# A hybrid transformer on one core: a changed order of routing, splits and the overflow branch, and constant matmuls at the experts' end

## The reference

```python
for i in range(DEPTH):                       # two layers
    mix = token_mixers(x, ...)               # x @ w_in, differential attention, attention over
                                             # the top 64 keys by an index score, gates, w_out
    x = layer_norm(ALPHA * x + mix, ln1_g[i], ln1_b[i])
    ffn = hierarchical_moe(x, ...)           # 4 groups of 8 experts; 2 experts of one group a token
    ple = jax.nn.sigmoid(x @ w_ple_gate[i]) * (p[i] @ w_ple[i])
    x = layer_norm(ALPHA * x + ffn + ple, ln2_g[i], ln2_b[i])
```

## Time and profile before

| | |
|---|---|
| median of 3 runs | 2013.76 us (2011.25 to 2013.92) |
| the profiled execution, its own time | 2016.33 us |
| its span, first to last instruction | 2014.2 us |
| PE busy | 1908.9 us (95%) |
| VectorE busy | 1406.5 us (70%) |
| ScalarE busy | 1073.4 us (53%) |
| mean granted clock of PE | 0.975 |

### The profile page before, as it was taken

The page is one execution under the profiler, slowest core; times in us unless marked ns, Lnnn a source line. Parts: engine busy times, 40 slices in busy tenths (PEclk is TensorE's granted clock), DMA queues, the critical chain, the costliest instruction groups (busy, mean ns, idle before and its releaser), DMA issues.

```text
span 2014.2 us, 31129 instructions
## 1 busy us (share of the span) xinstructions
PE 1908.9 (95%) x12576; PEld 1746.1 (87%) x12576; DVE 1406.5 (70%) x2285; ACT 1073.4 (53%) x1680; POOL 65.7 (3%) x78
## 2 busy tenths in 40 slices
PE   7899989999989999899998799999999999999998
PEld 6789879989878898799897689998998889998997
DVE  5876779888669767788886666676445666676444
ACT  5454557777544545677774445445444544444442
POOL 1000000000000000000000000000000000000001
PEclk9999989999899999899998899999999999999999
DMA  7426169999544252799993343445555343345552
GB/s 290 138 84 232 58 244 404 384 407 421 214 167 148 105 218 72 305 404 373 421 421 149 115 167 115 152 153 174 199 189 184 131 157 137 126 176 180 188 189 84
DMA packets 61049, 426.76 MB, mean 212 GB/s; under 512 B 6960, under 2 KB 7088, under 8 KB 11872
## 3 DMA queue, kind: packets, MB, share of 16 engines
q1 hardware_dynamic: 59760, 421.65, 55.5%
q0 software_dynamic: 416, 1.81, 0.3%
q10 hardware_dynamic: 720, 1.19, 0.2%
HBM read 423.58 MB, written 1.05 MB: 211 GB/s over the span
## 4 chain that ended last, share of the span: by engine, by line
PE 78%; DVE 13%; ACT 4%; DMA 3%; issue 1%; POOL 1%; DVEq 0%; ACTq 0%; SPq 0%; POOLq 0%
PE bank L1060 63%; PE scp L1060 10%; DVE WSl L1406 4%; ACT WSh L1971 1%; PE bank L1279 1%; PE bank L1156 1%; ACT SC L2020 1%; DMA PT<-wts 1%; DMA H<-wts 1%; PE bank L1139 1%; DVE sm L1554 1%; POOL sm L2208 1%; PE bank L1183 1%; PE bank L1299 1%; DMA A<-wts 1%
## 5 line engine op out<-in xcount | busy, mean ns | idle before, releaser
L1406 DVE TENSOR_TENSOR WSl<-ring,WSh 128x1024 fp32r<-128x1024 f32 (+3 forms) x512 | 590.3, 1197 | 203.4 <-ACT WSh L1971 202.1
L1971 ACT CAST WSh<-ring 128x1024 fp32r<-128x1024 f32 (+3 forms) x512 | 499.2, 1029 | 191.0 <-PE bank L1060 98.2
L1060 PE MATMUL bank<-XTh,WSh 128*128 128x256 f32 x1216 | 349.6, 288 | 7.2 <-DVE A L1589 4.4
L1060 PE MATMUL bank<-XTl,WSh 128*128 128x256 f32 x1216 | 345.9, 284 | 0.0
L1060 PE MATMUL bank<-XTh,WSl 128*128 128x256 f32 x1216 | 345.8, 284 | 0.0
L1060 PE MATMUL bank<-WSh,FA 128*128 128x512 f32 (+1 forms) x848 | 303.5, 391 | 6.2 <-DVE FA L1863 6.1
L1060 PE MATMUL bank<-WSl,FA 128*128 128x512 f32 (+1 forms) x680 | 263.2, 387 | 0.0
L1060 PEld LDWEIGHTS bank<-XTh,WSh 128*128 128x128 f32 x1216 | 234.9, 193 | 9.6 <-issue 5.4
L1060 PEld LDWEIGHTS bank<-XTl,WSh 128*128 128x128 f32 x1216 | 235.2, 193 | 0.2
L1060 PEld LDWEIGHTS bank<-XTh,WSl 128*128 128x128 f32 x1216 | 234.9, 193 | 0.0
L1060 PE MATMUL bank<-WSh,XTh 128*128 128x512 f32 (+4 forms) x544 | 204.2, 375 | 14.3 <-DVE WSl L1406 11.1
(11 more groups left out here) (285 smaller groups left out, 2906.8 us busy)
## 6 DMA issues: line engine op xcount, KB each, us to landing
ring<-wts SPq DMA_DIRECT2D x264, 1024.0 KB, 4.9
V<-wts SPq DMA_DIRECT2D x40, 1024.0 KB, 12.4
PT<-wts SPq DMA_DIRECT2D x30, 1024.0 KB, 9.1
H<-wts SPq DMA_DIRECT2D x28, 1024.0 KB, 9.5
GT<-wts SPq DMA_DIRECT2D x12, 1024.0 KB, 13.2
A<-wts SPq DMA_DIRECT2D x8, 1024.0 KB, 7.5
ring<-wts SPq DMA_DIRECT2D x8, 584.0 KB, 7.1
ring<-wts SPq DMA_DIRECT2D x4, 832.0 KB, 7.7
```

What stands on the lines that cost most here:

```text
L1060: return nc.tensor.matmul(dst, lhsT, rhs, start=start, stop=stop)
L1406: nc.vector.tensor_tensor(lo[:, c], buf[:, c], hi[:, c].bitcast(F32), ALU.subtract).then_inc(*lo_done.inc(("block", i)))
L1971: nc.scalar.copy(hi[:, c], buffers[s.buffer][:, c]).then_inc(*hi_done.inc(("half", i, k)))
```

## The change

Six places of the program's order are edited. None adds or removes arithmetic of the result; four plain matmuls on constants, whose bank nobody reads, are new in each layer.

1. `keep_on(4)`: between `turn_h` of the last expert and `down(31)`, PE multiplies the identity by the table `CST`, 4 times, 128x256 in fp32.
2. The waits in front of the overflow branch (four banks and the last scatter for PE, the last scatter for ScalarE) move into the branch's body, which is skipped when the flag is zero.
3. In the routing the blocks ahead are no longer split in the last two `parts` blocks (`limit` 0) but after `slots`; `affine` of tile 1 stands behind the first half of `gather`, and the late routing steps behind `turn_h` of expert 0.
4. `mix` of tile 0 stands in front of the split of the next block.
5. `pace` is 3 and not 8 in the dv columns, so fewer index steps come between two blocks.
6. `normed` of ln1 stands behind `ple_out` of the first two blocks.

```diff
@@ take() @@
         self.specs.append(spec)
+        self.ahead(i, spec)
+        self.spread_out(self.pace)
+        return i
+
+    def ahead(self, i, spec):
         order = self.order
...
                 self.give_back(j)
-        self.spread_out(self.pace)
-        return i
@@
+    def keep_on(self, n):
+        self.add("keep_on", n=n, u=self.bank("pe"))
@@ attend() @@
         if att == "diff":
-            self.fill(fills[0])
             self.add("mix", name=att, l=l, t=0)
-        else:
-            self.fill(fills[0])
+        self.fill(fills[0])
@@ first_layer @@
         self.add("rope", name="dq", l=l)
+        self.pace = 3
         self.columns("w_in", "dv", l, W1["dv"], 512, src)
@@
-        self.add("normed", name="ln1", l=l, n=D)
+        self.limit = 0
         i = self.take(("w_ple", (l,), 0, 2, 0, D))
+        self.limit = 3
...
-        for c in range(3):
+        for c in range(2):
             ple(c)
+            ple_out(c)
+        self.add("normed", name="ln1", l=l, n=D)
+        self.ahead(i, self.specs[i])
+        ple(2)
         xt = self.use("XT", "pe")
-        ple_out(0)
-        ple_out(1)
@@
                 self.add("ranks", l=l, u=self.bank("dve"))
+            self.limit = 0 if c >= 4 else 3
             blocks[c]()
@@
         self.add("slots", l=l, i=i, p=self.use("P", "pe"))
+        self.limit = 2
+        self.ahead(len(self.specs) - 1, self.specs[-1])
+        self.limit = 3
         self.add("spread", name="ln1", l=l, scp=self.use("scp", "dve"))
-        self.affine("ln1", l)
+        self.affine("ln1", l, (0,))
         for k in range(KD):
...
-            if k == KD - 1:
-                for n in ROUTE_LATE:
-                    for t in range(T):
-                        self.add("route", l=l, t=t, n=n)
-                self.add("kept", l=l)
+            if k == 3:
+                self.affine("ln1", l, (1,))
@@
             self.add("turn_h", l=l, e=e, u=self.bank("dve"))
+            if e == 0:
+                for n in ROUTE_LATE:
+                    for t in range(T):
+                        self.add("route", l=l, t=t, n=n)
+                self.add("kept", l=l)
             self.spread_out(1)
         self.pace = 1
+        self.keep_on(4)
         self.down(l, NE - 1)
@@ overflow_tensor @@
             with e.If(yes > 0):
                 pe, o_pe = Waiter(e), over[l]["pe"]
+                for v in range(u - 4, u):
+                    pe.wait_ge(emptied(v), "bank", v)
+                pe.wait_ge(dve_done, "added", "moe", l, 1, 1)
@@ overflow_scalar @@
                 act, o_act = Waiter(e), over[l]["act"]
+                act.wait_ge(dve_done, "added", "moe", l, 1, 1)
@@ PE's steps @@
+                elif s.kind == "keep_on":
+                    bank_free(u)
+                    for _ in range(s.n):
+                        last = mm(bank[u % 4][:, 0:256], ident, CST[:, 0:256], True, True)
+                    last.then_inc(*pe_done.inc(("bank", u)))
@@
                 elif s.kind == "overflow":
-                    for v in range(u - 4, u):
-                        pe.wait_ge(emptied(v), "bank", v)
-                    pe.wait_ge(dve_done, "added", "moe", l, 1, 1)
-                    overflow_tensor(e, l, yes)
+                    overflow_tensor(e, l, yes, u)
@@ ScalarE's steps @@
                 elif s.kind == "overflow":
-                    act.wait_ge(dve_done, "added", "moe", l, 1, 1)
                     overflow_scalar(e, l, yes)
```

More of the change, by code:

```diff
@@ L933, in overflow_pool, with overflow_tensor @@
                 pool.wait_ge(over[l]["dve"], "end", l)
-        def overflow_tensor(e, l, yes):
+        def overflow_tensor(e, l, yes, u):
             with e.If(yes > 0):
                 pe, o_pe = Waiter(e), over[l]["pe"]
+                for v in range(u - 4, u):
+                    pe.wait_ge(emptied(v), "bank", v)
+                pe.wait_ge(dve_done, "added", "moe", l, 1, 1)
                 def free(n):
```

## The result

The changed kernel takes 1995.74 us (median of 4 runs, 1994.76 to 1997.55) against 2013.84 (4 runs): ratio 0.9907, 95% interval 0.9884 to 0.9930. The profiled executions (2016.33 and 1996.55) lie 19.8 apart.

What follows compares the result with a forecast made beforehand. PE, busy 95% of the span, was taken as the bound, so only its idle, half-clock and late stretches could win. Terms -6.6 - 3.1 + 7.6 - 5.0 + 0 - 1.3 = -8.4 us gave 2005.4 us, range 1997 to 2014.

Steps and rivals of the forecast that it cites:

- the lowest sum of bounds: Whole kernel: every term at its most favourable bound, -17.3 us, giving 1996.5 us; left out of the range.
- Routing, +7.6: Routing to expert 2: fetch into `H` released later, costing 3.2 us in layer 0, 4.4 in layer 1; bounds +4.3, +10.
- Constants, -6.6: Experts' end: constant matmuls hold PE's clock, `down(31)` gains 5.7 us together, `turn_ys` 0.4 a layer; bounds +3.4, -8.4.
- Rival A: Experts' end: constants don't hold the clock and delay `down(31)`, +3.4 in place of -6.6, 2015.4 us; chance 0.14.
- Branch, -3.1: Overflow branch: PE jumps earlier and its code fetch is hidden, -2.4 us in layer 0, -0.7 in layer 1.
- Rival D: Branch: ScalarE's and VectorE's own jumps end last, so -0.3 in place of -3.1, 2008.2 us; chance 0.17.
- ln1, -1.3: ln1, both layers: PE's wait for the copy to `GT` goes, next chain about 0.65 us earlier; bounds -0.3, -2.
- Mix, 0: `mix`: idle moves to tile 1; -0.8 us a layer if the clock holds, +0.35 if it falls, taken as 0.
- dv columns, -5.0: Layer 0's dv columns: bank freed 3.3 to 3.4 us earlier, clock holding gives another 1.6; at least -3.4.
- Experts, 0: Experts behind the routing: PE sets the pace, so nothing is won back there, 0 us.
- Rival B: Routing costs nothing because the fetches catch up: 7.6 us off, 1997.8 us; chance 0.12.
- C: Rival: experts become bound by fetches, +0.3 us for each of some 58, +17.4, 2022.8 us; chance 0.05.

Runs made afterwards that it cites:

- first pair: First profiled executions of the kernel before and the changed kernel, compared stretch by stretch: 2016.33 and 1996.55 us.
- late_front: Changed kernel with only the late routing steps put back in front of expert 1's splits: 1996.24 us, ratio 0.9907 to the kernel before.
- no_constants: Changed kernel without its four constant matmuls: 2004.21 us, ratio 0.9948 to the kernel before.
- branch_alone: Kernel before with only the branch edit (waits moved into the skipped body): 2008.87 us, ratio 0.9987.
- warm_counts: Kernel before with four constant matmuls on PE right behind the counts' matmuls: 2012.88 us, ratio 0.9996.
- second pair: One more profiled execution each of the kernel before and the changed kernel, both unchanged, compared stretch by stretch; no total time is given.

## Why the prediction was wrong

The direction was right and the mechanisms named were mostly those seen; the sum of -8.4 was less than half of what came, and the lowest sum of bounds (-17.3) was just missed. The largest single step that failed is the clock of the last `parts` block in the routing, 3.6 of the 11.4 us between the forecast and the first pair. The rest is many terms, nearly all off to the same side. By steps:

- **Routing, +7.6: the step that failed most.** The sum took the last `parts` block "at mean clock 0.70 as before", though the same step shortens PE's wait in front of it from 2.04 to 0.47 us in layer 0. The block took 4.08 us at 1.00 and not 5.65, so it ends 1.6 us earlier in each layer; the lower bound of +4.3 was then the right value (+4.0 in both pairs). In layer 1 the wait was short before too (0.54 us), and why the clock fell there before and not after stays open. The rest of the chain was right: 11.55 us to the release predicted and 11.3 measured, 11.35 to expert 1 and 11.4 measured, 21.1 to expert 2 and 20.9. But the second profile has 0.62 over the block's start in layer 0: behind a wait of 0.47 us at the counts the clock was 1.00 in 26 of 27 cases. What edit 3 costs when it is undone in the changed kernel is less, 1.9 by medians. The 11.35 us to expert 1 came out right for a wrong reason: it had the late steps out of expert 1's way, and they were worth nothing (`late_front`), since in the new order VectorE waits there anyway.
- **Constants, -6.6: -8.3 and -8.2 in the two pairs, 8.5 by `no_constants`.** `turn_ys` was counted with 0.4 us a layer of a possible 1 to 1.5, and had all of it: with constants the clock was 1.00 behind the gap of 0.77 us after `down(31)` in 27 of 30 cases, without them 0.50 to 0.58 in 10 of 10. Rival A fell.
- **Branch, -3.1: -4.5 and -5.5 in the pairs, 2.6 when made alone, 2.9 when undone.** That the size is near is in part luck. The early jump itself is worth 2.5 to 2.8 us in the changed order, 1.1 to 1.3 in layer 0 and 1.5 in layer 1, where 0.7 was forecast. The stall of 1.86 us was priced as PE's own jump, and that reading failed: it is gone as well with the jump late and more instructions in front of it. Rival D (the branch brings nothing) fell.
- **ln1, -1.3: -2.0 in both pairs, 4.6 when undone (2.9 and 4.0 at ln1 in the two traces).** The row showed a wait, and I priced the chain behind it; that the clock can fall behind such a wait was not in the price, because in this trace it had not. It had in layer 0 of two other executions with the order before (0.68 in `branch_alone`, 0.63 in `warm_counts`).
- **Mix, 0: -1.8 and -1.5 in the pairs, 0.8 when undone.** The two cases of the prediction, the clock holds at tile 1 or it falls, are what the executions show, and not a mean of them: it fell in 11 of 14 executions with the new order and no constants there, and the fall costs 1.8 us in layer 0. The -1.5 of the first pair in layer 0 is chance: the changed kernel lost those 1.8 us, and the kernel before was 2.1 us slower than in its second execution, with the clock down at a place that the edit doesn't touch (0.56 over the 4 us from 152.68, 1.00 in the second).
- **dv columns, -5.0: -5.2 and 6.0.** Right, step by step.
- **Experts, 0: -2.4 in the first pair, +0.1 in the second.** Late transfers of that one execution of the kernel before.

Rival B (the fetches catch up) and C (experts bound by fetches) both fell: in the second pair the shift over 29 experts is 0 and +0.1.

## What to carry to other kernels

When an edit fills or removes a wait, price the stretch behind it at the clock that goes with the new wait, not with the old one; here the misses at the routing (3.6 us) and at `turn_ys` (1.7) were that, and both on one side. In a stretch that ends in a transfer, find the one instruction that releases the transfer and put everything that can wait behind it: putting two `affine`s in front of four split halves brought 10.5 us, more than any edit of the change. Constants that fill a gap of PE pay only where PE's stretch behind it sets the end: 8.5 us at the experts' end, nothing at the counts, and at `mix` about 1 us a layer in the trace. And before a difference of two traces is put down to an edit, compare two executions of one kernel over the same stretch: here they differ by up to 2.1 us.

## What the runs showed of the hardware

The granted clock behind a short gap isn't fixed by the kernel, but some places are far likelier to keep it than others. Over all 20 profiled executions, the mean over the 4 us behind the gap:

| place | gap, us | cases | below 1.00 |
|---|---|---|---|
| counts | 0.47 | 27 | 1 |
| `turn_ys`, with constants before `down(31)` | 0.77 | 30 | 3 |
| `turn_ys`, without | 0.77 | 10 | 10 |
| scores at the start | 1.31 | 20 | 5 |
| ln1, order before | 1.83 | 12 | 5 |
| mix of tile 1, layer 0, changed order, no constants | 1.83 | 14 | 11 |
| `down(31)`, without constants | 1.87 | 10 | 10 |
| `down(31)`, behind two constants | 1.00 | 2 | 0 |

The length of the gap alone doesn't order them: 0.77 us behind a slow `down(31)` was always followed by about half clock, and 0.77 behind a fast one seldom. One profile is no ground for a clock behind gaps of under 2 us.

Runs of one kernel differ by 2 to 12 us (2011.19 to 2023.56 for the kernel before on one chip). Losses of 0.5 to 2.5 us, by a clock that falls behind one of these gaps or by a transfer that comes late in the experts, are seen in single executions.
